# Scan stage of the gated linear attention: scores of the second direction masked ahead of the first direction's states, and the first four modulation products moved ahead of the second updates

## The chip, the cores and the metric

One core of one Trainium2 chip runs the whole program. The metric is the device time of one execution in microseconds (us); of several executions the median is taken. The engines are PE (TensorE, matrix products, with PEld for its weight loads), DVE (VectorE), ACT (ScalarE), POOL (GpSimd) and SP (SyncE, which here only issues DMAs).

## The reference, cut to what matters

The program is two transformer blocks. The change lies in one branch of the second block: gated linear attention in chunks of 64 tokens, with 8 heads and two directions, over 512 tokens and 256 tokens of context. For each head and direction it computes:

```python
bc = jnp.cumsum(logf, axis=3)
ref = bc[..., CHUNK // 2:CHUNK // 2 + 1, :]
scores = jnp.einsum('bhnid,bhnjd->bhnij', q * jnp.exp(bc - ref), k * jnp.exp(ref - bc))
scores = jnp.where(incl, scores, 0.0)
o_intra = jnp.einsum('bhnij,bhnjv->bhniv', scores, v)
q_dec = q * jnp.exp(bc)
k_dec = k * jnp.exp(bc[..., -1:, :] - bc)
tot = jnp.exp(bc[..., -1, :])
def step(S, xs):
    qd_c, kd_c, v_c, tot_c = xs
    o_c = jnp.einsum('bhcd,bhdv->bhcv', qd_c, S)
    S = tot_c[..., :, None] * S + jnp.einsum('bhcd,bhcv->bhdv', kd_c, v_c)
    return S, o_c
```

The outputs of both directions are added, normalised and gated. Beside it the same stage computes, for later use, eight column blocks of the modulation: `silu(c) @ w_ada` for `c` and for `c_ctx`.

## The kernel before

`scan_phase` holds the stage. It runs in periods `p` from -1 to 9, and each engine has a loop over the periods written out by hand, so the order in the code is the order of the engine's queue. Semaphores, counted by the helper `Marks`, tie the engines together: `VS.after(pe, "pt_f", h)` makes PE wait until DVE has reached the mark `pt_f` of head `h`. The marks of one `Marks` count upwards in one order, so the list of names has to be in the order in which the engine issues them. The letter `f` stands for the first direction, `b` for the second. In a period DVE, PE and ACT work on head `p`, and some of the work for heads `p + 1`, `p - 1` and `p - 2` stands between.

In a period, PE's order is:

- `turn_keys(p, 0)`: six transposes of the decayed keys (L2578); `scores(p, 0)` (L2599) into the one PSUM bank `ptb`, named `gla_scores` in the profile;
- `updates(p, 0)`: eleven products of keys and values (L2616), one per chunk, into the banks `kvb` (`gla_kv`);
- `turn_keys(p, 1)`, `scores(p, 1)`, which waits until DVE has read the first direction's scores out of `ptb`;
- `turn_values(p + 1)` (L2586);
- `updates(p, 1)`, which waits for the last state of the first direction, since both directions use the same `kvb` banks;
- `modulate(p, 0)`: four of eight modulation products (L2643), which also go into `ptb`, and so wait for `pt_b`;
- `outputs(p)`: for each direction four products with the masked scores `pt` (L2624) and eight with the states (L2628); each direction waits for its own last state;
- `modulate(p, 1)`, the other four; `sums(p)` (L2635).

DVE's order: `norm(p - 2)` (L2742), `decayed(p, 0)` (decayed keys `kd` L2709, `ke` L2712, `qe` L2715), `gated(p - 2)` (L2748), `decayed(p, 1)`, `visible(p, 0)`, `states(p, 0)`, `visible(p, 1)`, `lengths(p + 1)` (L2688), `states(p, 1)`, and twice `sums_of_logs(p + 1, r)` (`bc` L2695, `dm` L2699, `dl` L2701). `visible(h, r)` copies the visible scores out of `ptb` (L2721, mark `pt`) and makes the decayed queries `qd` (L2723). `states(h, r)` is a chain of one copy (L2733) and ten dependent steps (L2736) over the chunks; it waits for all eleven updates of its direction.

ACT copies the turned keys to SBUF (`kdt`, L2515), makes the exponentials for head `p + 1` (`e4` L2496, `e2` L2499, `e1` L2502), and then for head `p` squares and copies the outputs (`sq` L2521, `oc` L2522); next in its queue is `inv` for head `p - 1` (L2541), on which DVE's `norm` waits at the head of the next period. `take_ada` (L2536) moves the modulation products out of `ptb`; `scores(p + 1, 0)` waits for it.

SP loads the inputs of the heads to come. The modulation weights of head `p + 1` (`w_ada`, 2,048 KB, two buffers, L2404) are issued in period `p`, behind the loads of head `p + 2`. At the start of the stage POOL issues 32 DMAs of 768 KB that fill `gate_matrix` with zeros (L2455).

Of the kernel before, what the change touches and what calls it, by code (L numbers as in the profile page):

```python
# [2316 lines left out]
def scan_phase(nc, d):  # L2317
# [3 lines left out]
    R = ("f", "b")  # L2321
# [5 lines left out]
    with Scope(nc, "gla") as s:  # L2327
# [35 lines left out]
        steps = lambda x: [f"s{c}_{x}" for c in range(NCH - 1)]  # L2363
        VG = Marks(s.sem("dve_gates"), ["k_f", "k_b"] + [f"{n}_{r}" for r in R for n in ("bc", "dm", "dl")])
        VS = Marks(s.sem("dve_scan"), [f"{n}_{r}" for r in R for n in ("kd", "ke", "qe")]
                   + [n for r in R for n in [f"pt_{r}", f"qd_{r}"] + steps(r)])
        VE = Marks(s.sem("dve_end"), ["o1", "o2"])
        AG = Marks(s.sem("act_gates"), ["sg_f", "sg_b", "q", "lf_f", "lf_b", "v0", "v1"])
        AS = Marks(s.sem("act_scan"), ["e4_f", "e2_f", "e1_f", "e4_b", "e2_b", "tot_f", "tot_b", "kdt0_f", "kdt1_f",
# [6 lines left out]
        TO = Marks(s.sem("pe_out"), ["out", "sumsq"])  # L2376
# [189 lines left out]
        def _(pe):  # L2566
# [3 lines left out]
            def turn_keys(h, r):  # L2570
                VS.after(pe, f"kd_{R[r]}", h)
                for n, (a, b) in enumerate(spans):
                    if r:
                        AS.after(pe, f"kdt{n}_f", h)
                    else:
                        AG.after(pe, f"v{n}", h)
                    for c in range(a, b):
                        last = pe.transpose(tr[n][:, c - a], kd[r][:, c * P:(c + 1) * P], ident[:])  # L2578
                    TS.mark(f"tk{n}_{R[r]}", h, last)

            def turn_values(h):
                pe.wait_ge(loaded["i"], 16 * (h + 1))
                for n, (a, b) in enumerate(spans):
                    AS.after(pe, f"kdt{n}_b", h - 1)
                    for c in range(a, b):
                        last = pe.transpose(tr[n][:, c - a], iz[:, c * P:(c + 1) * P], ident[:])  # L2586
                    TG.mark(f"tv{n}", h, last)

            def scores(h, r):
                x = R[r]  # L2590
                VS.after(pe, f"qe_{x}", h)
                if r:
                    VS.after(pe, "pt_f", h)
                else:
                    VS.after(pe, "pt_b", h - 1)
                    need(pe, ada_taken, h)
                for c in range(4):
                    for lo, part in windows[r]:
                        last = pe.matmul(ptb[lo:lo + 32, c, part], ke[r][:, c * P + lo:c * P + lo + 32],  # L2599
                                         qe[r][:, c * P + part.start:c * P + part.stop], start=True, stop=True)  # L2600
                TS.mark(f"scores_{x}", h, last)

            def updates(h, r):
                x = R[r]
                AS.after(pe, f"kdt1_{x}", h)
                AG.after(pe, "v1", h)
                if r:
                    VS.after(pe, f"s{NCH - 2}_f", h)
                else:
                    VS.after(pe, f"s{NCH - 2}_b", h - 1)  # L2610
                for n in range(2):
                    if n:
                        TS.after(pe, f"kv0_{x}", h)
                    for c in sorted(chunks[r][:-1])[(n + r) % 2::2]:
                        half = slice(c % 2 * CHUNK, c % 2 * CHUNK + CHUNK)
                        last = pe.matmul(kvb[c // 4][:, c % 4], kdt[r][half, c // 2], v[h % 2][half, c // 2], start=True, stop=True)  # L2616
                    TS.mark(f"kv{n}_{x}", h, last)

            def outputs(h):
                AO.after(pe, "oc", h - 1)  # L2620
                for r in dirs:
                    VS.after(pe, f"s{NCH - 2}_{R[r]}", h)
                    for c in range(4):
                        pe.matmul(ob[:, c * P:(c + 1) * P], v[h % 2][:, c], pt[r][:, c], start=r == 0 and c == 0, stop=False,  # L2624
                                  skip_group_check=True)
                    for c in range(NX):
                        part = slice(c * CHUNK, (c + 1) * CHUNK)
                        last = pe.matmul(ob[:, part], state[r][:, c], qd[r][:, part], start=False, stop=r == 1,  # L2628
                                         skip_group_check=True)
                TO.mark("out", h, last)  # L2630

            def sums(h):
                AO.after(pe, "sq", h)
                AN.after(pe, "lno", h - 1)
                TO.mark("sumsq", h, pe.matmul(ssb[:], ones[:], sq[:], start=True, stop=True))  # L2635

            def modulate(i, part):
                pe.wait_ge(w_ada_loaded[i % 2], 16 * (i // 2 + 1))
                if part == 0:
                    pe.wait_ge(silu_made, 1)  # L2640
                    VS.after(pe, "pt_b", i)
                for c in range(DC // 2 * part, DC // 2 * (part + 1)):
                    last = pe.matmul(ptb[0:2].rearrange("p c n -> p (c n)"), silu_c[:, c], w_ada[i % 2][:, c], start=c == 0, stop=c == DC - 1)  # L2643
                if part:
                    last.then_inc(ada_products, 1)

            for p in PERIODS:
                if head(p):
                    turn_keys(p, 0)
                    scores(p, 0)  # L2650
                    updates(p, 0)
                    turn_keys(p, 1)
                    scores(p, 1)
                if head(p + 1):
                    turn_values(p + 1)
                if head(p):
                    updates(p, 1)
                    modulate(p, 0)
                    outputs(p)
                    modulate(p, 1)  # L2660
                    sums(p)
# [9 lines left out]
        def _(ve):  # L2671
# [45 lines left out]
            def visible(h, r):  # L2717
                x = R[r]
                TS.after(ve, f"scores_{x}", h)
                TO.after(ve, "out", h - 1)  # L2720
                VS.mark(f"pt_{x}", h, ve.copy_predicated(pt[r][:], mask[r][:].unsqueeze(1).to_broadcast([P, 4, P]).bitcast(U32), ptb[:]))  # L2721
                AS.after(ve, f"e3_{x}", h)
                VS.mark(f"qd_{x}", h, ve.tensor_tensor(qd[r][:], q[h % 2][:], e3[r][:], ALU.mult))  # L2723

            def states(h, r):
                x = R[r]
                AS.after(ve, f"tot_{x}", h)
                TS.after(ve, f"kv1_{x}", h)
                for n, c in enumerate(chunks[r][:-1]):
                    kv = kvb[c // 4][:, c % 4]  # L2730
                    nxt = state[r][:, chunks[r][n + 1]]
                    if n == 0:
                        ins = ve.tensor_copy(nxt, kv)  # L2733
                    else:
                        VS.after(ve, f"s{n - 1}_{x}", h)
                        ins = ve.scalar_tensor_tensor(nxt, state[r][:, c], tot[r][:, c:c + 1], kv, ALU.mult, ALU.add)  # L2736
                    VS.mark(f"s{n}_{x}", h, ins)

            def norm(h):
                AE.after(ve, "inv", h)  # L2740
                AO.after(ve, "oc", h)
                VE.mark("o1", h, ve.scalar_tensor_tensor(o1[:], oc[h % 2][:], DK_SCALE, inv[:], ALU.mult, ALU.mult))  # L2742

            def gated(h):
                VE.after(ve, "o1", h)
                AN.after(ve, "gate", h)
                need(ve, stored, 16 * h)
                VE.mark("o2", h, ve.scalar_tensor_tensor(o2[:].rearrange("p (r w) -> p w r", w=GRID_W), by_columns(o1[:]), nw[:, 0:1],  # L2748
                                                         by_columns(gate[:]), ALU.mult, ALU.mult))

            for p in PERIODS:
                if head(p - 2):
                    norm(p - 2)
                if head(p):
                    decayed(p, 0)
                if head(p - 2):
                    gated(p - 2)
                if head(p):
                    decayed(p, 1)
                    visible(p, 0)  # L2760
                    states(p, 0)
                    visible(p, 1)
                if head(p + 1):
                    lengths(p + 1)
                if head(p):
                    states(p, 1)
                if head(p + 1):
                    sums_of_logs(p + 1, 0)
                    sums_of_logs(p + 1, 1)
# [708 lines left out]


PHASES = (mixer_phase, route_phase, expert_phase, input_phase, delta_phase, scan_phase, last_phases)  # L3480


# [88 lines left out]
```

## Time and profile before

| | |
|---|---|
| median of 3 runs | 4636.1 us (4633.9 to 4636.14) |
| the profiled execution: its time | 4634.58 us |
| the profiled execution: its span | 4632.9 us |
| mean granted TensorE clock over the span | 0.956 |
| PE busy | 4200.1 us (91%) |
| DVE busy | 3208.1 us (69%) |
| ACT busy | 2022.8 us (44%) |
| the scan stage, first to last period | about 2900 to 3160 us |

The profile is of one execution. "Span" is the time from its first to its last instruction, 1.7 us less than the time of that execution. The timeline gives the start, the length and the kind of each group of instructions in order of time; behind them, in brackets, the idle time of the engine before the group and what ended it. The view by stretches gives for each stretch how long each engine was busy and the granted TensorE clock as a share of full speed (1.00 is 2.4 GHz, 0.50 is 1.2 GHz).

### The profile page before, as it was taken

How to read it: one execution, taken by the hardware profiler on the slowest of the kernel's cores; microseconds unless marked ns; L12 is line 12 of the kernel's file. 1: busy time of each engine (PE TensorE's matmuls, PEld its weight loads, DVE VectorE, ACT ScalarE, POOL GpSimd, SP SyncE). 2: the span in 40 equal slices, each digit the busy share in tenths (PEclk: the TensorE clock that was granted, in tenths of full speed). 3: DMA queues.
4: the chain of work that ended last, by engine and by line, in shares of the span. 5: the costliest groups of instructions: out<-in, count | busy, mean ns of one | idle time of the engine just before them, and what ended most of it. 6: DMA issues, size and time to landing. Idle time of an engine off the chain costs nothing. (4 is left out here: it accounts for less than half of the span.)

```text
span 4632.9 us, 60088 instructions
## 1 busy us (share of the span) xinstructions
PE 4200.1 (91%) x22088; PEld 3499.0 (76%) x22088; DVE 3208.1 (69%) x4487; ACT 2022.8 (44%) x2378; POOL 958.3 (21%) x836
## 2 busy tenths in 40 slices
PE   8987999999999669999778888798899999899997
PEld 3345777777777558888668878456699999888886
DVE  6226998888888652223288886784378895599998
ACT  1115767776767431101156564664344333233332
POOL 1010000000000110000000000200047787566664
PEclk9988999999999889999889999788899999999999
DMA  9347999999999633334410110935254545899997
GB/s 353 143 161 301 363 367 368 366 368 373 367 368 363 260 123 111 108 111 143 128 46 26 37 33 8 365 131 185 88 163 155 155 156 172 310 411 410 411 409 302
DMA packets 289651, 1067.20 MB, mean 230 GB/s; under 512 B 45636, under 2 KB 98452, under 8 KB 235636
## 3 DMA queue, kind: packets, MB, share of 16 engines
q1 hardware_dynamic: 226772, 854.53, 50.0%
q0 software_dynamic: 62688, 210.11, 11.5%
q8 instruction: 121, 1.98, 0.2%
q14 instruction: 70, 0.57, 0.0%
HBM read 912.04 MB, written 152.45 MB: 230 GB/s over the span
## 5 line engine op out<-in xcount | busy, mean ns | idle before, releaser
L1189 DVE TENSOR_TENSOR moe_low<-moe_raw,moe_high 128x2048 fp32r<-128x2048 f32 x256 | 574.6, 2287 | 55.8 <-ACT moe_high L1097 53.0
L3415 ACT ACTIVATE peer_high<-peer_raw 128x1024 fp32r<-128x1024 f32 x272 | 288.0, 1059 | 448.5 <-DMA peer_raw<-expert_v 403.7
L1097 ACT ACTIVATE moe_high<-moe_raw 128x2048 fp32r<-128x2048 f32 x256 | 477.9, 1904 | 3.5 <-DMA moe_raw<-w_gate_up 3.5
L3340 POOL DMA_INDIRECT gate_matrix<-peer_whole_gate,peer_cell x336 | 399.3, 1188 | 107.5 <-issue 106.0
L3092 DVE TENSOR_TENSOR peer_low<-peer_raw,peer_high 128x1024 fp32r<-128x1024 f32 x272 | 331.6, 1220 | 125.9 <-ACT peer_high L3415 125.4
L84 PE MATMUL peer_bank<-peer_hidden_high,peer_high 128*128 128x384 f32 x1024 | 353.9, 346 | 63.7 <-DVE peer_hidden_low L3213 63.2
L84 PE MATMUL peer_bank<-kept_t_high,peer_high 128*128 128x384 f32 (+1 forms) x1152 | 393.5, 342 | 9.2 <-DVE peer_low L3092 9.2
L85 PE MATMUL peer_bank<-kept_t_low,peer_high 128*128 128x384 f32 (+1 forms) x1152 | 392.7, 341 | 0.0
L86 PE MATMUL peer_bank<-kept_t_high,peer_low 128*128 128x384 f32 (+1 forms) x1152 | 392.6, 341 | 0.0
L77 DVE CAST zin_both_w_high<-zin_both_w 128x1024 fp32r<-128x1024 f32 x88 | 61.0, 694 | 422.8 <-DMA zin_both_w<-w_in 422.8
L86 PE MATMUL peer_bank<-peer_hidden_high,peer_low 128*128 128x384 f32 x1024 | 344.8, 337 | 0.0
L85 PE MATMUL peer_bank<-peer_hidden_low,peer_high 128*128 128x384 f32 x1024 | 344.6, 337 | 0.0
L1194 DVE TENSOR_TENSOR moe_low<-moe_raw,moe_high 128x2048 fp32r<-128x2048 f32 x128 | 293.0, 2289 | 66.2 <-ACT moe_high L1102 66.2
L84 PE MATMUL zin_tokens<-zin_hT_high,zin_both_w_high 128*128 128x512 f32 x704 | 276.8, 393 | 6.5 <-DVE zin_hT_low L1433 5.9
L86 PE MATMUL zin_tokens<-zin_hT_high,zin_both_w_low 128*128 128x512 f32 x704 | 277.0, 393 | 0.0
L85 PE MATMUL zin_tokens<-zin_hT_low,zin_both_w_high 128*128 128x512 f32 x704 | 275.6, 392 | 0.0
L84 PEld LDWEIGHTS peer_bank<-peer_hidden_high,peer_high 128*128 128x128 f32 x1024 | 193.5, 189 | 97.8 <-DVE peer_low L3092 64.9
L1382 POOL MEMSET zin_ident<- 128x128 f32 x1 | 0.2, 205 | 1227.7 <-POOLq L103 1227.7
L1102 ACT ACTIVATE moe_high<-moe_raw 128x2048 fp32r<-128x2048 f32 x128 | 244.1, 1907 | 0.8 <-DMA moe_raw<-w_down 0.7
L84 PEld LDWEIGHTS peer_bank<-kept_t_high,peer_high 128*128 128x128 f32 x1152 | 216.7, 188 | 15.1 <-issue 8.6
L3345 POOL DMA_INDIRECT peer_ring<-expert_v,peer_expert x128 | 200.2, 1564 | 107.2 <-DVE peer_y L3231 82.0
L1005 PE MATMUL moe_gate_bank<-moe_high,moe_x_high 128*128 128x512 f32 x512 | 210.0, 410 | 12.6 <-DVE moe_low L1189 12.6
(585 smaller groups left out, 10232.5 us busy)
## 6 DMA issues: line engine op xcount, KB each, us to landing
moe_raw<-w_gate_up SPq DMA_DIRECT2D x256, 1024.0 KB
moe_raw<-w_down SPq DMA_DIRECT2D x128, 1024.0 KB, 7.6
peer_raw<-expert_u SPq DMA_DIRECT2D x128, 512.0 KB
peer_raw<-expert_v SPq DMA_DIRECT2D x128, 512.0 KB
zin_both_w<-w_in SPq DMA_DIRECT2D x88, 512.0 KB, 3.8
rows<-mix_zero POOLq DMA_DIRECT2D x12, 2048.0 KB, 14.3
gate_matrix<-gla_zeros POOLq DMA_DIRECT2D x32, 768.0 KB, 41.4
hidden<-peer_gelu SPq DMA_DIRECT2D x128, 192.0 KB, 1.9
```

The costliest lines, as they stand in the source:

```text
L84: pe.matmul(out, wh, xh, start=start, stop=False)
L85: pe.matmul(out, wh, xl, start=False, stop=False)
L86: return pe.matmul(out, wl, xh, start=False, stop=stop)
L1005: pe.matmul(out[:], sh[:, c], w[:, part][:, q * 512:(q + 1) * 512], start=False, stop=False, skip_group_check=True)
L1097: act.activation(high[:, gu_slot[j]], raw[:, gu_slot[j]], ACT.Copy).then_inc(gu_high, 1)
L1102: act.activation(high[:, dn_slot[j]], raw[:, dn_slot[j]], ACT.Copy).then_inc(dn_high, 1)
L1189: v.tensor_tensor(low[:, slot], raw[:, slot], high[:, slot].bitcast(F32), ALU.subtract).then_inc(gu_low, 1)
L1194: v.tensor_tensor(low[:, slot], raw[:, slot], high[:, slot].bitcast(F32), ALU.subtract).then_inc(dn_low, 1)
L3092: v.tensor_tensor(low_part[:, slot], raw[:, slot], high[:, slot].bitcast(F32), ALU.subtract).then_inc(cut_low, 1)
L3340: pool.indirect_dma_start(out=cells, out_offset=at_cell, in_=source[:, t, h * TOPK + k:h * TOPK + k + 1], in_offset=None).then_inc(scatter ...
L3345: pool.indirect_dma_start(out=ring[:, n % RING], out_offset=None, in_=rows, in_offset=bass.IndirectOffsetOnAxis(ap=expert[:, j:j + 1], axi ...
L3415: act.activation(high[:, k % 4], raw[:, k % 4], ACT.Copy).then_inc(cut_high, 1)
```

## The change

Two things move, in every one of the eight periods with a head, and the list of DVE's marks follows them. On DVE, `visible` is split: its masked copy (`pt`) stays, and the decayed queries become `decayed_q`. The second direction's masked copy now stands ahead of the first direction's states; its decayed queries stand behind them. On PE, `modulate(p, 0)` stands ahead of `updates(p, 1)`. No instruction is added or removed on either engine, and no DMA.

```diff
-                   + [n for r in R for n in [f"pt_{r}", f"qd_{r}"] + steps(r)])
+                   + ["pt_f", "qd_f", "pt_b"] + steps("f") + ["qd_b"] + steps("b"))
...
                 if head(p):
+                    modulate(p, 0)
                     updates(p, 1)
-                    modulate(p, 0)
                     outputs(p)
                     modulate(p, 1)
                     sums(p)
...
                 VS.mark(f"pt_{x}", h, ve.copy_predicated(pt[r][:], mask[r][:].unsqueeze(1).to_broadcast([P, 4, P]).bitcast(U32), ptb[:]))
+
+            def decayed_q(h, r):
+                x = R[r]
+                TO.after(ve, "out", h - 1)
                 AS.after(ve, f"e3_{x}", h)
                 VS.mark(f"qd_{x}", h, ve.tensor_tensor(qd[r][:], q[h % 2][:], e3[r][:], ALU.mult))
...
                 if head(p):
                     decayed(p, 1)
                     visible(p, 0)
+                    decayed_q(p, 0)
+                    visible(p, 1)
                     states(p, 0)
-                    visible(p, 1)
+                    decayed_q(p, 1)
                 if head(p + 1):
                     lengths(p + 1)
```

PE's queue in the second half of the first period, before and now (names as in the profile: `gla_iz` are the values, `gla_kdt` the turned keys, `gla_w_ada` the modulation weights):

```order
 L2599 MATMUL gla_scores<-gla_qe,gla_ke 32x64
 L2586 MATMUL gla_transposes<-gla_ident,gla_iz 128x128 x6
+L2643 MATMUL gla_scores<-gla_w_ada,gla_silu_c 2x512 x4
 L2616 MATMUL gla_kv<-gla_v,gla_kdt 128x128 x11
-L2643 MATMUL gla_scores<-gla_w_ada,gla_silu_c 2x512 x4
 L2624 MATMUL gla_out<-gla_pt,gla_v 128x128 x4
 L2628 MATMUL gla_out<-gla_qd,gla_state 128x64 x8
```

Four modulation products have changed places with the eleven updates of the second direction; the outputs now follow the updates directly.

DVE's queue in the same period (the change's lines are 4 to 6 higher in number from here on):

```order
 L2721 COPY_PREDICATED gla_pt<-gla_mask,gla_scores 128x512
-L2723 TENSOR_TENSOR gla_qd<-gla_q,gla_e 128x512
-L2733 COPY gla_state<-gla_kv 128x128
-L2736 SCALAR_TENSOR_TENSOR gla_state<-gla_state,gla_tot,gla_kv 128x128 x10
+L2727 TENSOR_TENSOR gla_qd<-gla_q,gla_e 128x512
 L2721 COPY_PREDICATED gla_pt<-gla_mask,gla_scores 128x512
-L2723 TENSOR_TENSOR gla_qd<-gla_q,gla_e 128x512
+L2737 COPY gla_state<-gla_kv 128x128
+L2740 SCALAR_TENSOR_TENSOR gla_state<-gla_state,gla_tot,gla_kv 128x128 x10
+L2727 TENSOR_TENSOR gla_qd<-gla_q,gla_e 128x512
 L2688 TENSOR_SCALAR gla_k<-gla_sg,gla_lbm,gla_oml 128x768 x2
```

The second masked copy has moved from behind the first direction's eleven state instructions to ahead of them; both decayed queries keep their side of the states.

## Rows read from the trace of the kernel before

**Rows 1.** The page's first line.

```profile
span 4632.9 us, 60088 instructions
```

**Rows 2.** Stretches from one first-direction masked copy to the next: three of seven.

```profile
core 0: us, PE busy (x) PEld busy (x) DVE busy (x) ACT busy (x) POOL busy (x), PEclk, DMA share, GB/s
2954.86:2982.93 28.07, 25.73 (x196) 16.53 (x193) 23.38 (x44) 20.27 (x32) 0.00 (x0) 0.88 1.02 401
...
3040.42:3070.10 29.68, 27.18 (x193) 16.75 (x193) 23.30 (x43) 19.98 (x32) 0.00 (x0) 0.83 0.37 138
...
3098.12:3126.12 28.00, 25.50 (x193) 16.29 (x193) 23.30 (x43) 19.98 (x32) 0.00 (x0) 0.88 0.24 89
```

**Rows 3.** Timeline of DVE in one period: start, length, line, operation, [idle before].

```profile
3012.42 0.73 DVE L2721 COPY_PREDICATED gla_pt<-gla_mask,gla_scores 128x512 f32<-128x512 uint32 x1
3013.63 0.29 DVE L2733 COPY gla_state<-gla_kv 128x128 f32<-128x128 f32 x1
...
3017.66 0.73 DVE L2721 COPY_PREDICATED gla_pt<-gla_mask,gla_scores 128x512 f32<-128x512 uint32 x1
...
3022.54 0.29 DVE L2733 COPY gla_state<-gla_kv 128x128 f32<-128x128 f32 x1 [2.40 <-PE gla_kv L2616]
...
3026.58 1.75 DVE L2695 TENSOR_TENSOR_SCAN gla_bc<-gla_keep,gla_lf 128x768 f32<-128x768 f32 x1
...
3034.72 0.69 DVE L2742 SCALAR_TENSOR_TENSOR gla_o<-gla_oc,gla_inv 128x512 f32<-128x512 f32 x1 [1.54 <-ACT gla_inv L2541]
3035.33 0.95 DVE L2709 TENSOR_TENSOR gla_kd<-gla_k,gla_e 128x768 f32<-128x768 f32 x1
```

**Rows 4.** Timeline of PE in the same period.

```profile
3011.01 2.36 PE L2616 MATMUL gla_kv<-gla_v,gla_kdt 64*128 64x128 f32 x22 [0.17 <-ACT gla_kdt L2515]
...
3014.11 0.65 PE L2599 MATMUL gla_scores<-gla_qe,gla_ke 128*32 128x32 f32 x32
...
3017.80 4.69 PE L2616 MATMUL gla_kv<-gla_v,gla_kdt 64*128 64x128 f32 x22 [2.22 <-DVE gla_state L2736]
3022.43 5.12 PE L2643 MATMUL gla_scores<-gla_w_ada,gla_silu_c 128*2 128x512 f32 x8
3027.47 1.16 PE L2624 MATMUL gla_out<-gla_pt,gla_v 128*128 128x128 f32 x8
...
3030.20 1.11 PE L2624 MATMUL gla_out<-gla_pt,gla_v 128*128 128x128 f32 x8
3031.15 1.90 PE L2628 MATMUL gla_out<-gla_qd,gla_state 128*128 128x64 f32 x16
3032.98 3.59 PE L2643 MATMUL gla_scores<-gla_w_ada,gla_silu_c 128*2 128x512 f32 x8
3037.46 0.82 PE L2578 MATMUL gla_transposes<-gla_ident,gla_kd 128*128 128x128 f32 x6
```

**Rows 5.** Timeline of ACT at the end of the same period.

```profile
3031.22 0.61 ACT L2502 ACTIVATE gla_e<-gla_dm 128x512 f32<-128x512 f32 x1
...
3033.08 0.60 ACT L2521 ACTIVATE gla_sq<-gla_out 128x512 f32<-128x512 f32 x1 [1.25 <-PE gla_out L2628]
```

**Rows 6.** Stretches with the granted clock (the figure ahead of the last two), period 3 (from 3018.80) and period 0.

```profile
3018.80:3022.40 3.60, 3.54 (x16) 3.05 (x14) 1.34 (x3) 3.56 (x5) 0.00 (x0) 0.50 0.86 292
...
3025.60:3028.00 2.40, 2.40 (x9) 0.78 (x8) 2.33 (x4) 0.51 (x1) 0.00 (x0) 1.00 0.95 398
...
2933.40:2936.80 3.40, 2.93 (x23) 2.49 (x22) 2.97 (x6) 3.35 (x5) 0.00 (x0) 1.00 1.02 375
2936.80:2940.20 3.40, 3.40 (x7) 0.67 (x6) 2.62 (x8) 3.39 (x4) 0.00 (x0) 0.50 0.99 307
```

**Rows 7.** The issue of the second modulation weights, and SP's queue (q1) between 2956 and 2964 us.

```profile
2938.43 1.59 SPq L2404 DMA_DIRECT2D gla_w_ada<-w_ada  x1
...
q1 hardware_dynamic: 3, 0.03, 1.0%
```

**Rows 8.** Timeline of PE, the last head: the second half of its modulation products.

```profile
3148.28 3.60 PE L2643 MATMUL gla_scores<-gla_w_ada,gla_silu_c 128*2 128x512 f32 x8
```

## The prediction

> **What bounds the kernel now.** I read the stage first by stretches, one per head, from one masked copy of the first direction to the next. Six such stretches lie between 2954.86 and 3126.12 us, 171.3 us together, or 28.5 us a head; they last 28.0 to 29.7 us [rows 2]. PE is busy for 25 to 27 us of each, but at a mean granted clock of 0.83 to 0.88 [rows 2], so its busy time is no floor. DVE, with 23.3 us, and ACT, with 20.0 us, are not full either. What sets the period has to be read as a chain, in the timeline of one head. I count from the start of its first masked copy, 3012.42 us, as T.
>
> DVE's states of the first direction run from T+1.2 to about T+5.3 (3013.63 to the next operation's start at 3017.66) [rows 3]. PE has nothing to do for 2.22 us and waits for them; only then does it start the second updates, at T+5.4 [rows 4]. The second states wait 2.40 us more for those, start at T+10.1, and hand over to the scan of the logarithms at T+14.2 [rows 3]. Meanwhile PE does the four modulation products and the outputs, which end at T+20.6 (3031.15 + 1.90) [rows 4]. ACT waits for the outputs, squares, copies and makes `inv` [rows 5]; DVE waits 1.54 us for that, and the next head begins [rows 3]. So the chain is: first states, second updates, modulation, outputs, ACT, DVE.
>
> Behind the idle 2.22 us PE is slow. The same 22 matmul records take 2.36 us in the first updates and 4.69 us in the second; the eight records of modulation take 5.12 us behind those and 3.59 us at the end of the period [rows 4]. The granted clock is 0.50, which is the level of 1.2 GHz, from 3018.80 to 3022.40, and 1.00 again by 3025.60 [rows 6]. One idle gap thus costs 2.33 + 1.53 = 3.9 us of PE time on the chain, on top of the gap.
>
> **The masked copy moved ahead.** It keeps its 0.73 us but now waits for the second direction's scores. Those end at 3014.76, T+2.3 [rows 4], while DVE is free at T+1.2. Before, though, PE started the key transposes at 3037.46, 2.1 us after the decayed keys began at 3035.33 [rows 3, 4], since modulation and sums stood in its queue; if PE is done earlier, they start once the keys are finished, 0.95 us after their start, and the updates follow as soon as ACT has copied. I take 0.7 us of this to reach the scores, so they end at T+1.6. The states of the first direction then start at about T+2.3 and end at T+6.4: 1.1 us later than before, or 1.8 us if PE is not earlier. That is the price of the change. Each decayed query stays beside waits: the second one and the two lengths, about 1.9 us, lie between the states, where DVE had 2.40 us idle, and will have 2.4 us.
>
> **The modulation moved ahead.** It can start when the masked copy is done and the value turns are through, T+2.4. At full clock it takes 3.6 us, to T+6.0, and the second updates can go at T+6.4. The idle 2.22 us become 0.4 us. Taking the full clock there, the updates take 2.36 us, to T+8.8, instead of ending at T+10.1. The second states start at T+8.85 instead of T+10.1: 1.27 us gained here, the gap filled and the clock kept, less the masked copy. The scan of the logarithms starts at T+12.9 instead of T+14.2.
>
> **The outputs.** They no longer stand behind modulation. The first direction's part (3027.47 to 3030.20, 2.7 us [rows 4]) runs from T+8.8 to T+11.5; then PE waits for the second states until T+13.0, a new gap of 1.45 us; the second part (2.85 us) ends at T+15.85, against T+20.6 before. That is 4.8 us earlier, and outputs are off the chain. What is late next is ACT's exponentials: from the start of the scan to the end of the third one are 3031.22 + 0.61 - 3026.58 = 5.25 us, so ACT is free for the squares at about T+18.05. From there to DVE's norm it was 34.72 - 33.08 = 1.64 us, and from norm to the next masked copy 3040.42 - 3034.72 = 5.70 us [rows 2, 3, 5]. The new period is 12.89 + 5.16 + 1.64 + 5.70 = 25.4 us. DVE's own queue would give 25.2, and PE needs about 22.5 us at full clock. The second half of modulation and the sums end at about T+20.4, 0.9 us before the next keys are ready.
>
> **The ends.** In period 0 there is no norm, and DVE already waits elsewhere; following the chain through gives a gain of 0.3 us. In period 1 the keys come later, and I get 26.4 us. In the last head the second modulation half ended at 3148.28 + 3.60 = 3151.88, T+25.8 [rows 8]; now T+19.35, 6.4 us less, and the tail moves with it. Sum with the clock kept: 171.3 - (26.4 + 5 x 25.4) = 17.9, plus 6.4 and 0.3, is **24.6 us gained**.
>
> **What the new gap costs.** The trace has no gap of 1.45 us in this stage. Bounds: nothing, if the clock stays; 3.9 us, the price of today's gap, less the 0.9 us that PE has to spare at the period's end, is 3.0 us a head. Neither 0 nor 3.0 in all heads is nearest: 1.45 lies between 2.22 us, after which the clock falls in every head, and the short gaps of at most a few tenths, after which it mostly does not. Once, it did even then: from 2933.40 to 2936.80 PE had the full clock and was idle for only 0.47 us, beside updates, and the stretch behind it ran at 0.50 [rows 6]. So where the gap lies matters. I take two heads of eight: 6 us given back. That leaves 18.6 us. The Trainium skill (TensorE: Matmul & The Clock Gate, "A second HAM failure mode") says that PE pauses between groups of matmuls, each short, can make the clock swing between its levels; by that rule two short gaps in place of one long one would lose all of it, rival one below. The row at 2933.40 is on its side.
>
> **Sum.** From the profiled execution, 4634.6 us (its span of 4632.9 us [rows 1] and 1.7 us around it), less 18.6 gives 4616.0. The median of the runs is 1.5 us above that execution: 4617.5 us. What comes behind the stage, 1,470 us, starts earlier and keeps its length; I grant it 2 us either way, for the clock's changes fall elsewhere in it.
>
> **Rivals.** One: the clock falls in the new gap, in every head. Eight times 3.0 gives 24 of the 24.6 us back: about 4635.5 us, no change that a measurement can tell (0.2%, 9.3 us, is about what one can). For it: updates and outputs with a pause between are close to what stood before the fall at 2936.80. Against: in the second half of the period, outputs at full clock for 5.6 us never lost it. Chance 0.12.
>
> Two, the other side: modulation weights late. Modulation now stands ahead of the second updates, so a late load stops the updates, the states and the outputs behind them. Modulation of head 1 began in the kernel before 27 us after the load's issue at 2938.43 and did not wait; now it wants the weights at about 2958, 19.6 us after it. If the load needs the whole 27 us, PE waits 7.4 us for it; later heads leave 25.4 us less some 6 us from issue to use, so they wait 7.6. In the three heads in which the zeros are still being written, with the clock falling before the products (3.9 us more) and the 3.1 us of gain, each head is then 8.4 us longer than before: 25.2 against the remaining 3 x 3.1 + 6.4 = 15.7, so 9.5 us slower; 4645.6 us. It decides from 20 us after issue. Against: the hardware queue moves only 0.03 MB between 2956 and 2964 [rows 7], so the 2 MB had landed by 2956, 17.6 us after issue, and 2 us of margin are left. Chance 0.04.
>
> Three: the clock stays everywhere: 4636.1 - 24.6 = 4611.5 us. Chance 0.25; it is the lower part of my own range. Four: the reordering does what it says, but the masked copy waits the longer 1.8 us and PE is never earlier; 0.7 us a head less, and falls in four heads: 24.6 - 5 - 12 = 7.6, 4628.5 us. Chance 0.15. The forecast itself, falls in one to three heads: 0.44.
>
> **The numbers.** 4617.5 us. The range goes from 4609 (clock kept, and 2 us more) to 4630 (rival four and a little). Faster by over 0.2%, that is below 4626.8: the forecast, rival three and a good half of rival four, with a little of what I have not thought of: 0.80. Within: 0.15. Slower: 0.05.
>
> **What would show it.** Right: the wait of the second updates for the states at 0.4 us or less, those updates at 2.4 us; masked copies one behind the other at T and about T+1.65; the first states from T+2.3; a gap of PE ahead of the second direction's outputs of 1.4 us; ACT's squares no longer waiting for PE; periods of 25.4 us, and near 28.5 us where the clock fell. Wrong: PE waiting at the modulation products, a clock below 1.00 in most heads, or periods of 28 us with the full clock.

## The result, and the profile after

The changed kernel takes 4628.2 us (median of 20 runs, 4619.8 to 4636.0), the kernel before 4636.1 us in the 20 runs beside it (4628.8 to 4643.1). The ratio is 0.9983, with a 95% interval of 0.9977 to 0.9989: 7.9 us faster. The forecast was 18.6 us faster, and the result lies within the 0.2% that I had called the limit of what one can tell; with this many runs it can be told, but it is less than half of what was forecast.

The page of the changed kernel, its first line and the granted clock in 40 slices:

```profile
span 4630.5 us, 60088 instructions
...
PEclk9988999999999889999989999799899999999999
```

The span is only 2.4 us shorter than in [rows 1], since one profile scatters by some us outside the stage: the stage's first PE instruction starts at 2912.29 us here and started at 2907.22 us before, 5.1 us later, and what stands behind the stage took 2.8 us more. So I measure the stage by itself, from that instruction to the first product of the merge behind it. For each kernel, timeline of PE, first row before, second row after:

```profile
2907.22 1.51 PE L2586 MATMUL gla_transposes<-gla_ident,gla_iz 128*128 128x128 f32 x6 [14.92 <-DMA gla_iz<-zT]
...
3171.62 0.77 PE L84 MATMUL merge_bank<-merge_oa_high,merge_high 128*128 128x512 f32 x1 [10.65 <-DVE merge_oa_low L2816]
```

```profile
2912.29 1.51 PE L2586 MATMUL gla_transposes<-gla_ident,gla_iz 128*128 128x128 f32 x6 [15.22 <-DMA gla_iz<-zT]
...
3166.42 0.76 PE L84 MATMUL merge_bank<-merge_oa_high,merge_high 128*128 128x512 f32 x1 [10.66 <-DVE merge_oa_low L2822]
```

The stage takes 264.4 us before and 254.1 us after: 10.3 us gained in this profile.

The changed kernel by stretches, from one first masked copy to the next, answers to [rows 2]. The first row is head 0, then heads 1 to 6; the figure ahead of the last two is the granted clock:

```profile
2931.55:2965.07 33.52, 31.84 (x203) 20.45 (x202) 21.84 (x42) 18.47 (x29) 0.96 (x2) 0.72 1.02 397
```

```profile
2965.07:2992.19 27.12, 24.00 (x206) 15.33 (x203) 23.43 (x44) 20.15 (x32) 0.00 (x0) 1.00 1.01 386
2992.19:3018.20 26.01, 22.88 (x194) 14.45 (x193) 23.43 (x43) 19.75 (x31) 0.75 (x1) 1.00 0.84 332
3018.20:3045.07 26.87, 24.75 (x183) 15.96 (x182) 23.49 (x43) 19.57 (x31) 0.00 (x0) 0.87 0.41 153
3045.07:3072.21 27.14, 24.02 (x206) 15.33 (x204) 23.45 (x44) 20.16 (x32) 0.00 (x0) 1.00 0.42 151
3072.21:3099.10 26.89, 24.76 (x183) 15.44 (x182) 23.48 (x44) 19.47 (x31) 0.00 (x0) 0.87 0.47 165
3099.10:3126.20 27.10, 24.93 (x200) 16.67 (x199) 23.40 (x43) 20.26 (x32) 0.00 (x0) 0.94 0.23 85
```

One head, the one from 2992.19 (T), passes with the full clock throughout and with a free PE at its start. It takes 26.0 us. DVE in it, against [rows 3]:

```profile
2992.19 0.74 DVE L2721 COPY_PREDICATED gla_pt<-gla_mask,gla_scores 128x512 f32<-128x512 uint32 x1
...
2993.79 0.73 DVE L2721 COPY_PREDICATED gla_pt<-gla_mask,gla_scores 128x512 f32<-128x512 uint32 x1 [0.28 <-PE gla_scores L2599]
2994.41 0.28 DVE L2737 COPY gla_state<-gla_kv 128x128 f32<-128x128 f32 x1
...
3001.65 0.29 DVE L2737 COPY gla_state<-gla_kv 128x128 f32<-128x128 f32 x1 [1.35 <-PE gla_kv L2616]
...
3005.69 1.75 DVE L2695 TENSOR_TENSOR_SCAN gla_bc<-gla_keep,gla_lf 128x768 f32<-128x768 f32 x1
...
3012.47 0.69 DVE L2746 SCALAR_TENSOR_TENSOR gla_o<-gla_oc,gla_inv 128x512 f32<-128x512 f32 x1 [0.17 <-ACT gla_inv L2541]
```

ACT's squares no longer wait for PE (timeline of ACT, against [rows 5]; no bracket, so no idle time before it):

```profile
3010.86 0.57 ACT L2521 ACTIVATE gla_sq<-gla_out 128x512 f32<-128x512 f32 x1
```

And PE in it, against [rows 4]:

```profile
2989.85 2.36 PE L2616 MATMUL gla_kv<-gla_v,gla_kdt 64*128 64x128 f32 x22
...
2994.67 3.59 PE L2643 MATMUL gla_scores<-gla_w_ada,gla_silu_c 128*2 128x512 f32 x8
2998.58 3.04 PE L2616 MATMUL gla_kv<-gla_v,gla_kdt 64*128 64x128 f32 x22 [0.32 <-DVE gla_state L2740]
...
3005.83 1.16 PE L2624 MATMUL gla_out<-gla_pt,gla_v 128*128 128x128 f32 x8 [1.40 <-DVE gla_state L2740]
...
3008.65 3.59 PE L2643 MATMUL gla_scores<-gla_w_ada,gla_silu_c 128*2 128x512 f32 x8
...
3014.09 0.87 PE L2578 MATMUL gla_transposes<-gla_ident,gla_kd 128*128 128x128 f32 x6 [0.79 <-DVE gla_kd L2709]
```

Nearly all is as forecast: the copies at T and T+1.6, the first states from T+2.2, modulation from T+2.5 in 3.6 us, the second updates at T+6.4, a gap of 1.40 us in the outputs. One row is not: the second updates take 3.04 us at the full clock, where the sum had 2.36.

Not every head has PE free at its start. In heads 1, 4 and 6 the second masked copy stands 2.7 us behind the first, not 1.6, because it waits 1.40 us for the second scores; those heads take 27.1 us at a clock of 1.00, 1.00 and 0.94. The row of head 4, timeline of DVE:

```profile
3047.77 0.73 DVE L2721 COPY_PREDICATED gla_pt<-gla_mask,gla_scores 128x512 f32<-128x512 uint32 x1 [1.40 <-PE gla_scores L2599]
```

In three of the six later heads (3, 5 and 6), and in head 0, the clock falls in the outputs' gap, although that gap is 1.39 or 1.40 us long in all eight heads. In head 0 it looks so:

```profile
2946.86 1.90 PE L2628 MATMUL gla_out<-gla_qd,gla_state 128*128 128x64 f32 x16
2950.15 2.07 PE L2624 MATMUL gla_out<-gla_pt,gla_v 128*128 128x128 f32 x8 [1.40 <-DVE gla_state L2740]
2952.01 3.52 PE L2628 MATMUL gla_out<-gla_qd,gla_state 128*128 128x64 f32 x16
2955.46 6.05 PE L2643 MATMUL gla_scores<-gla_w_ada,gla_silu_c 128*2 128x512 f32 x8
```

Behind the gap the same 24 records of the outputs take 5.4 us and modulation 6.05 us, 11.4 us from 2950.15 to 2961.51, where the head above has 3005.83 to 3012.24, 6.4 us. The keys of the next head then wait for PE. The clock over this fall, by stretches:

```profile
2949.95:2960.75 10.80, 10.60 (x31) 6.00 (x32) 10.14 (x12) 4.33 (x7) 0.00 (x0) 0.53 1.02 416
```

So the theory (A) is now: the reordering does what it says; it fell short by two sizes, the second updates' 3.04 us and the number of heads in which the clock falls in the new gap. Each has a rival, and so has the change's own logic, that its two parts only pay together.

### The profile page after: what moved, and what is told of

It is laid out like the page before. It is cut to its first block and busy times, and to the rows that moved or that the text cites. A ratio compares the mean times of both kernels' runs of the same rounds, so it can differ in the third digit from the quotient of the medians.

```text
span 4630.5 us, 60088 instructions
## 1 busy us (share of the span) xinstructions
PE 4190.5 (90%) x22088; PEld 3496.9 (76%) x22088; DVE 3209.9 (69%) x4487; ACT 2021.9 (44%) x2378; POOL 959.3 (21%) x836
```

## Experiments

Each kernel was timed beside runs of the kernel before on the same chip. The stage and the periods are read from its one profile as above.

### Each part alone

The masked copy ahead of the first states, modulation where it was (a diff against the changed kernel):

```diff
-                    modulate(p, 0)
                     updates(p, 1)
+                    modulate(p, 0)
                     outputs(p)
```

> The masked copy moved, modulation left where it was. Theory A (two parts, the masked copy costs 1.1 to 1.8 us a head, the modulation in front pays for it by filling the gap and keeping the clock): PE then sits idle some 4 us ahead of the second updates instead of 2.2, the clock still falls in every head, the period is 29.6 to 30.3 us and the kernel 9 to 14 us slower than before. Rival B (the gain comes from the masked copy order itself, the second updates find the states sooner): no slower than before, periods of 28.5 us or less.

Measured: 4651.5 us against 4633.9; ratio 1.0038 (1.0024 to 1.0052), about 17.6 us slower, where A had 9 to 14. The periods of heads 1 to 6 are 30.7 to 31.1 us, also above what A gave, the clock falls in every head, and the stage takes 282.3 us. PE ahead of the second updates:

```profile
3025.49 5.49 PE L2616 MATMUL gla_kv<-gla_v,gla_kdt 64*128 64x128 f32 x22 [4.03 <-DVE gla_state L2740]
```

4.03 us idle and updates of 5.49 us: rival B is out. By itself, the masked copy's new place only costs.

Modulation ahead of the updates, the masked copy where it was (a diff against the kernel before):

```diff
+                    modulate(p, 0)
                     updates(p, 1)
-                    modulate(p, 0)
                     outputs(p)
```

> Modulation moved, the masked copy left behind the first states. Theory A: modulation waits for the masked copy until 6 us after the first one, the clock falls in that idle time, modulation takes 5 us or more and the second updates start some 6 us later than before; the scan of the logarithms starts 3.5 us later and the period is about 30.2 us, 12 to 14 us slower than before in all. Rival C (the order of modulation and updates alone brings the gain, since outputs then follow the updates directly): faster than before by 5 us or more.

Measured: 4649.2 us against 4633.9; ratio 1.0036 (1.0022 to 1.0050), about 15 us slower, a little more than A had, with periods of 29.4 to 31.7 us and a stage of 278.7 us. The first four modulation products in head 2, and the same with the updates behind them in head 3:

```profile
2990.84 3.59 PE L2643 MATMUL gla_scores<-gla_w_ada,gla_silu_c 128*2 128x512 f32 x8 [2.73 <-DVE gla_pt L2721]
...
3020.10 5.26 PE L2643 MATMUL gla_scores<-gla_w_ada,gla_silu_c 128*2 128x512 f32 x8 [3.78 <-DVE gla_pt L2721]
3025.30 3.04 PE L2616 MATMUL gla_kv<-gla_v,gla_kdt 64*128 64x128 f32 x22
```

Modulation waits for the masked copy in every head, and rival C is out too. But only half of A came true: the clock falls in this wait where it lasts 3.8 us or more (heads 3, 4, 5 and 7), and not in heads 1, 2 and 6, where it lasts 2.73 us and modulation takes 3.59 us. Head 2 keeps a clock of 1.00 throughout and still takes 29.35 us, against 28.5 us a head in the kernel before with a fall in each: the wait on the chain costs enough by itself. And a gap of 2.73 us without a fall stands against the kernel before, where 2.0 to 2.2 us made the clock fall each time: the length alone does not decide. What does was not tried; behind the gap stand the 512-wide modulation products here and the updates there. Each half of the change costs some 15 to 18 us, both together gain 8.

### The gap in the outputs

The second direction's products with the masked scores need no state, so they can go ahead of the wait:

```diff
                 for r in dirs:
-                    VS.after(pe, f"s{NCH - 2}_{R[r]}", h)
+                    if r == 0:
+                        VS.after(pe, f"s{NCH - 2}_f", h)
                     for c in range(4):
                         pe.matmul(ob[:, c * P:(c + 1) * P], v[h % 2][:, c], pt[r][:, c], start=r == 0 and c == 0, stop=False,
                                   skip_group_check=True)
+                    if r:
+                        VS.after(pe, f"s{NCH - 2}_b", h)
                     for c in range(NX):
```

> The changed kernel, with the second direction's four products with the masked scores ahead of the wait for the second states, so that the gap of 1.40 us in the outputs becomes about 0.45. Theory A (the clock falls in this gap, in 4 of 8 heads of the changed kernel, at about 2 us each): the clock falls in none of heads 1 to 7, all their periods are 26.0 us, and the stage is 6 to 8 us shorter than the 254.1 us of the changed kernel. Rival D (the clock falls for a reason that the gap has no part in, such as the updates themselves): falls as often, and at most 1 us is gained, since ACT's exponentials, not the outputs, set the period.

Measured: 4614.2 us against 4633.9; ratio 0.9955 (0.9942 to 0.9969), 19.7 us faster than before. Heads 2 to 5 all have 26.0 us and the stage takes 249.2 us, 4.9 less than the changed kernel's; A had 6 to 8. The gap is now 0.45 us and no fall begins in it. But the idle time has gone to the end of the head, and once the clock fell there, ahead of the keys:

```profile
3066.77 2.00 PE L2631 MATMUL gla_out<-gla_qd,gla_state 128*128 128x64 f32 x16 [0.45 <-DVE gla_state L2743]
...
3075.04 0.87 PE L2578 MATMUL gla_transposes<-gla_ident,gla_kd 128*128 128x128 f32 x6 [1.48 <-DVE gla_kd L2712]
3076.24 0.73 PE L2599 MATMUL gla_scores<-gla_qe,gla_ke 128*32 128x64 f32 x32 [0.33 <-DVE gla_qe L2718]
3076.90 4.11 PE L2616 MATMUL gla_kv<-gla_v,gla_kdt 64*128 64x128 f32 x22
```

That head takes 28.8 us. Two more falls came right behind the second updates, in heads 2 and 7, with only 0.32 and 0.41 us of idle time ahead of the updates. So D is out as far as the gap's part goes: no fall begins in the outputs, and the period without a fall is 26.0 us here as in the changed kernel, so earlier outputs by themselves gain nothing. But A was too narrow, for it had no fall at all in heads 1 to 7. The place moves with the gap, and the updates of one half may be a weak spot of their own: the fall of [rows 6] at 2936.80 was behind them too, and none of the profiles with mixed updates has one there.

The other filling, two modulation products in the gap, leaves the second outputs where they were. Cut to its core:

```diff
                 for r in dirs:
+                    if r:
+                        modulate(h, (4, 5))
                     VS.after(pe, f"s{NCH - 2}_{R[r]}", h)
...
                     outputs(p)
-                    modulate(p, 1)
+                    modulate(p, (6, 7))
                     sums(p)
```

> The changed kernel with two of the four late modulation products between the outputs of the two directions: the gap is filled with other work, and the second direction's outputs come no earlier. Theory A (the gap makes the clock fall): no falls in the outputs, as with the masked-score products in it; the stage 247 to 251 us. Rival D (that kernel was faster since its outputs ended a microsecond earlier): the stage stays at 253 to 256 us. PE will be idle for 1.8 us more later, ahead of the sums or the keys, and a fall may move there.

Measured: 4625.2 us against 4635.0; ratio 0.9983 (0.9974 to 0.9992), 9.8 us faster than before, and a stage of 259.7 us: longer than either had it. No fall is in the outputs any more, so the gap was their cause, but from head 3 on the clock falls ahead of the keys, and those periods are 28.8 to 29.4 us:

```profile
3026.42 1.12 PE L2637 MATMUL gla_sumsq<-gla_sq,gla_ones 128*128 128x512 f32 x2 [0.61 <-ACT gla_sq L2521]
3029.02 0.88 PE L2578 MATMUL gla_transposes<-gla_ident,gla_kd 128*128 128x128 f32 x6 [1.48 <-DVE gla_kd L2711]
...
3030.85 4.11 PE L2616 MATMUL gla_kv<-gla_v,gla_kdt 64*128 64x128 f32 x22
```

A fall there costs more than one in the outputs, 2.8 to 3.4 us above the 26.0, since scores and updates behind it lie on the chain. Neither figure for the stage was met, as the new falls hide what the filled gap gained; but head 2, in which the clock falls only at the very end, takes 26.0 us once more, though its outputs end 1.2 us later than those of the kernel above. That speaks against D too.

### The second updates

```diff
-                    for c in sorted(chunks[r][:-1])[(n + r) % 2::2]:
+                    for c in (sorted(chunks[r][:-1])[n::2] if r == 0 else ((2, 4, 6, 9, 11), (1, 3, 5, 7, 8, 10))[n]):
```

The first direction leaves out a chunk in the middle, so that taking every other one gives batches 0, 2, 4, 6, 9, 11 and 1, 3, 5, 8, 10: both parities, and a chunk's parity is the half of the 128 partitions that its product reads. The second direction's batches are all even and all odd.

> The changed kernel, with the eleven second updates in batches that take chunks of both halves of the partitions (2, 4, 6, 9, 11 and 1, 3, 5, 7, 8, 10), as those of the first direction do. Theory A (the second updates take 3.04 us and not 2.36 at full clock, because products of one partition half go one by one and those of two halves in pairs): they take about 2.4 us, the period without a fall is 25.4 us, and the kernel is 4 to 5.5 us faster than the changed one. Rival E (they are slower for what runs beside them, or for their place behind modulation): they stay at 3.0 us and nothing changes.

Measured: 4622.5 us against 4633.9; ratio 0.9973 (0.9963 to 0.9982), 11.4 us faster than before, some 3.5 us more than the change alone, though the two intervals overlap. The stage takes 251.6 us.

```profile
3042.10 2.36 PE L2616 MATMUL gla_kv<-gla_v,gla_kdt 64*128 64x128 f32 x22 [0.32 <-DVE gla_state L2740]
...
3048.67 1.21 PE L2624 MATMUL gla_out<-gla_pt,gla_v 128*128 128x128 f32 x8 [1.39 <-DVE gla_state L2740]
3049.68 3.52 PE L2628 MATMUL gla_out<-gla_qd,gla_state 128*128 128x64 f32 x16
```

2.36 us, to the digit the figure of the first updates: E is out. The edit leaves the order in which the PSUM banks are written as it was (banks 0, 1, 1, 2, 2, then 0, 0, 1, 1, 2, 2 in either order), so it is the halves and not the banks. The first batch of five products, timeline of PE, in one half in the changed kernel and mixed here:

```profile
2998.58 1.38 PE L2616 MATMUL gla_kv<-gla_v,gla_kdt 64*128 64x128 f32 x10 [0.32 <-DVE gla_state L2740]
```

```profile
3042.10 1.04 PE L2616 MATMUL gla_kv<-gla_v,gla_kdt 64*128 64x128 f32 x10 [0.32 <-DVE gla_state L2740]
```

In one half the records start 0.11 us apart, but for the first two; in the mixed batch three times a record starts within 6 ns of the one before it. In this profile, however, the clock falls in the outputs' gap in every head from head 2 on, and the periods of heads 3 to 6 are all 27.3 us. The one later head without a fall, head 1, takes 26.4 us, the figure that the prediction's sum had for it.

The same edit in the kernel before:

> The kernel before with the second updates in mixed halves. Theory A (products of two halves go in pairs, at either clock): the second updates take 0.7 to 1.3 us less than 4.4 to 5.5 us at the low clock, and since they lie on the chain, the kernel is 4 to 9 us faster than before. Rival E (pairs form only at the full clock): no difference.

Measured: 4622.7 us against 4635.0; ratio 0.9970 (0.9961 to 0.9980), 12.3 us faster: more than A had, more than the change under study gives, and as much as the change and the mixed updates give together (ratio 0.9973, above). With the updates mixed, then, the change by itself adds nothing that these runs can show; it pays only once the outputs' gap is filled as well. Pairs form at the low clock too. The updates take 4.11 us at the low clock, against 4.4 to 5.5 before; the periods are 27.3 us:

```profile
3017.99 4.11 PE L2616 MATMUL gla_kv<-gla_v,gla_kdt 64*128 64x128 f32 x22 [2.21 <-DVE gla_state L2736]
3022.03 4.97 PE L2643 MATMUL gla_scores<-gla_w_ada,gla_silu_c 128*2 128x512 f32 x8
```

The Trainium skill (TensorEngine Tiling (Array Packing), "Theoretical Speedup") gives up to twice the speed, by a tiling factor of 2, where the small dimension is 64 or less. The runs agree in kind: at the low clock 5.49 us in one half's order against 4.11 in the mixed one, at the full clock 3.04 against 2.36, which is 1.3 times, with only some of the products paired.

### Both cures, and the last gap

> The changed kernel once more, beside the three below on one chip. Theory A: periods of 26.0 us where the clock stays and some 27 us where it falls in the outputs' gap or fell in the head before; between 3 and 7 falls, in other heads than in the first profile, since only their timing against the clock's own steps decides; the stage 252 to 256 us; 0.1 to 0.25% faster than before.

Measured: 4628.0 us against 4635.0; ratio 0.9980 (0.9970 to 0.9990), the first result again. The stage takes 255.4 us. The falls lie in other heads: head 0 now passes at a clock of 0.99 in 26.2 us, where it had 33.5, and heads 1 to 4 have 27.9 to 29.6 us. So it is not the head that decides.

> Both cures together: the outputs' gap filled and the second updates in mixed halves. Theory A (the two causes add up): updates of 2.4 us, a gap of 0.45 us, at most one or two falls, periods of 25.4 us, which is the figure of the prediction's sum with the clock kept; the stage 240 to 245 us and the kernel 20 to 25 us faster than before. Rival F (what is gained in PE's part is given back, because with PE further ahead the idle time before the next keys grows and the clock falls there): the stage stays at 249 us or more.

Measured: 4610.7 us against 4635.0; ratio 0.9953 (0.9939 to 0.9968). The stage takes 243.7 us, and heads without a fall 25.32 us: the 25.4 of the prediction's sum. Two falls are left, both ahead of the keys, in periods of 28.0 and 28.2 us: rival F had the place of them right, but not their weight. In head 1 modulation already waits for its weights:

```profile
2961.22 3.60 PE L2646 MATMUL gla_scores<-gla_w_ada,gla_silu_c 128*2 128x512 f32 x8 [0.44 <-DMA gla_w_ada<-w_ada]
```

> Both cures once more, beside the split one on one chip. Theory A: periods of 25.3 us without a fall, 28 us with one ahead of the keys, one to four falls, the stage 240 to 248 us.

Measured in another series: 4616.8 us against 4632.5; ratio 0.9964 (0.9954 to 0.9974); three falls, stage 247.4 us. Its nine runs lie between 4604.4 and 4623.0.

The last experiment cuts up the idle time that is left at the end of the head:

```diff
                     outputs(p)
-                    modulate(p, 1)
+                    modulate(p, (4, 5, 6))
                     sums(p)
+                    modulate(p, (7,))
```

> Both cures, and the last of the eight modulation products behind the sums, so that PE's idle time at the end of a head comes as about 0.9 us ahead of the sums and 0.5 us ahead of the keys, not as 1.5 us ahead of the keys. Theory A (a gap of about 1.4 us makes the clock fall in part of the heads wherever it lies, shorter ones hardly): no fall after the first head, all periods 25.3 us, the stage 237 to 241 us, and the kernel 2 to 6 us faster than both cures alone. Rival G (the idle time of a whole head decides, however it is cut): falls stay, the stage 243 us or more.

Measured: 4608.9 us against 4632.5; ratio 0.9950 (0.9936 to 0.9963), 23.6 us faster than before, and 7.9 us ahead of both cures alone in the same series (6.5 us by the two ratios, whose intervals overlap). Against the first series of both cures, at 0.9953, it is ahead by only 1.4 us. The five runs lie within 3.8 us (4606.8 to 4610.6). The profile shows no fall in all eight heads (the one low stretch left, from 3129.5 us, lies behind the last head's products), a stage of 237.2 us, and five periods of 25.33 or 25.34 us in a row. Two stretches of it, and PE at the end of a head:

```profile
2979.36:3004.69 25.33, 22.43 (x197) 13.71 (x196) 23.43 (x43) 19.77 (x31) 0.00 (x0) 1.00 1.02 409
3004.69:3030.02 25.33, 22.42 (x197) 13.69 (x196) 23.43 (x43) 19.77 (x31) 0.75 (x1) 1.00 0.59 215
```

```profile
3023.75 1.13 PE L2638 MATMUL gla_sumsq<-gla_sq,gla_ones 128*128 128x512 f32 x2 [0.99 <-ACT gla_sq L2521]
3024.80 1.02 PE L2646 MATMUL gla_scores<-gla_w_ada,gla_silu_c 128*2 128x512 f32 x2
3026.35 0.87 PE L2578 MATMUL gla_transposes<-gla_ident,gla_kd 128*128 128x128 f32 x6 [0.52 <-DVE gla_kd L2713]
```

PE is idle for as long as before in such a head; it is only cut into 0.99, 0.52 and some shorter pieces. Rival G is out, as far as one profile of each version goes. This is the best version of the study, and it beats both kernels.

## Why the prediction was wrong

**Right: the chain and its new order.** The states' delay of 1.1 us (measured 2.22 - 1.21 = 1.0), the filled gap, outputs off the chain with ACT and DVE as the next bound, and the new gap of 1.4 us all stand in the rows above; PE's 22.5 us a head at full clock was 22.9 with the slower updates and 22.4 with the mixed ones. The step from the scan to ACT's squares, which the prediction adds up to 5.25 us and then takes as 5.16, measured 5.17. The period of 25.4 us was never reached by the changed kernel, but by the kernels with both causes removed, at 25.3 us. The sum with the clock kept, 24.6 us, was nearly met by the last of them at 23.6, though that kernel has three more edits.

**Wrong in size: "Taking the full clock there, the updates take 2.36 us".** I took the duration of the first updates for the second, since both are 22 records of one shape. The kernel before never showed the second ones at the full clock outside its first head; there they took 3.23 us. The real figure is 3.04: 0.68 us more, because their batches read one half of the partitions each. This alone makes the period 26.0, and head 1, whose keys come later, 27.1 where the sum had 26.4.

**Wrong in size: "I take two heads of eight: 6 us given back".** Falls came in four of eight heads in the first profile and in six in the second. The price of 3.0 us was too high for later heads (0.9 us in the head itself and 1.1 us in the next, whose keys wait for PE: about 2 us) and too low for head 0. That head took 33.5 us, where the sum had 28.1 and the second profile 26.2. The kernel with the outputs' gap filled began head 0 with 7.2 us at the low clock, much as the changed kernel did (8.4 us), had no fall in it and took 28.5 us; so some 5 us of the 33.5 are the fall, which lasted 10.8 us.

The account against the sum with the clock kept: head 0 took 33.5 - 28.1 = 5.4 us more. Heads 1 to 6 took 161.1 us, where the sum had 26.4 + 5 x 25.4 = 153.4: 7.7 us more, of which 0.7 + 5 x 0.6 = 3.7 are the updates and 4.0 the three falls with the late keys behind them. From the last head's first masked copy to the merge it was 45.5 us before and 40.2 after, a gain of 5.3 where the sum had 6.4: 1.1 us. Together 14.2 us, where this profile fell short by 24.6 - 10.3 = 14.3; this takes the stage's own gain apart, and is no test of it. What the whole program gained is 7.9 us, a little less than the stage in either profile (10.3 and 9.0 us); that rest is not explained.

What the changed kernel leaves open is why the same gap of 1.40 us brings a fall in one head and not in another. The runs show that the falls go away from the outputs when the gap is filled, and no more.

**The rivals.** Rival one, a fall in every head and no gain, did not come, but lay as near as the forecast: I gave it 0.12, and what I had for it, the stretch at 2933.40 in [rows 6], was the better guide. The rule of the Trainium skill that I set beside it (TensorE: Matmul & The Clock Gate, "A second HAM failure mode") holds in part: with the pauses cut to 1.4 us the clock still swings, in half of the heads, but it did not lose all of the gain, and in the split version the shorter pauses brought no fall. Rival two, late modulation weights, did not come in the changed kernel, but its margin was misread. I took the load to have landed 17.6 us after its issue. In the kernels in which modulation of head 1 waited for it, it was there 19.3 to 19.9 us after its issue, and the wait was 0.44 and 0.75 us in the two profiles of both cures, 0.30 us with two modulation products in the gap, and 0.98 us in the split version. In its second profile the changed kernel used the weights 19.3 us after their issue: the margin was near nothing, and not 2 us. Rival four's figure, 4628.5 us, is the measured one, and its mechanism came in part. It had the masked copy waiting longer because PE is never earlier, and falls in four heads. PE was earlier, and the copy waited 0.28 us, in the heads with a free PE; in heads 1, 4 and 6 it waited 1.40 us, and four heads had a fall. What it left out is the updates' 3.04 us, so that its figure came so near is luck. The range ended at 4630 and held the result.

## What to carry to other kernels

A busy share at a mean clock below 1.00 hides two costs: work that runs slow, and the waits that make it slow. Before moving work into an idle gap of PE, list the gaps that remain and those that arise, with their lengths: here gaps of 2.0 to 2.2 us ahead of the updates made the clock fall in each head that had one, of 1.4 to 1.5 us in about half of them, and with 1.0 us and less in none of the last version's, though three times behind one-half updates with 0.3 to 0.4 us ahead of them. Length alone is no rule: 2.7 us ahead of modulation brought no fall in three heads. To cut one gap of 1.5 us into two was worth 1 to 8 us by the series that it is compared with. Remove the causes in the kernel before as well: with the updates mixed, the change under study had no gain left of its own. Take a duration only from rows of the same shape and the same operands' places: 22 equal records took 2.36 or 3.04 us by which half of the partitions they read.

## What was not expected of the hardware

Where a fall comes differs from one execution to the next, and yet it can repeat: with the mixed updates alone, four periods in a row had a fall and 27.3 us, and two profiles of one and the same kernel had head 0 at 33.5 and at 26.2 us. The scatter of the runs may go with falls that come in some heads only: it is 17.7 us from the lowest to the highest of 11 runs of the changed kernel, 18.6 us in nine of both cures, and 3.8 us in the five of the kernel that never lost the clock. This is not shown: the five runs of the masked copy alone, with a fall in every head, lie within 4.2 us, and those of the filled gap, with three falls, within 5.2. How much of the scatter before is from the other stages was not tried.
